# One change in three places of a two-layer decoder trunk: the attention's value products turned over, the router's products in column strips, and the first expert's tokens picked straight from x

## The reference

```python
def rmsnorm(x, g):
    y = xf * lax.rsqrt(jnp.mean(xf * xf, axis=-1, keepdims=True) + RMS_EPS)
    return y * g
# layer 0, attention: o_g = softmax(q k^T / 8, masked) v for 3 groups,
#   merged with weights softmax over groups of the log-sum-exps, then @ w_o
# layer 1, pooling mixer:
x = x + (window_mean(h) - h) @ w_group * scale
# layer 1, experts:
logits = h @ w_router                      # 256 x 8
top_val, top_idx = lax.top_k(logits, 2)
gates = softmax(top_val)
x = x + sum over the 2 chosen experts of gate * (silu(h Wg) * (h Wu)) Wd
```

## Time and profile before

| what | value |
|---|---|
| median of 3 runs | 1531.43 us |
| profiled execution | 1531.06 us, span 1529.3 us |
| PE busy | 1493.1 us (98%) |
| PEld busy | 1258.0 us (82%) |
| DVE busy | 1200.3 us (78%) |
| ACT busy | 965.2 us (63%) |
| attention | about 20 to 312 us of the span |
| dense layer | about 312 to 503 us |
| pooling, routing, first tokens | about 503 to 539 us |
| experts | about 539 to 1514 us |

### The profile page before, as it was taken

How to read it: one execution, slowest core, us unless ns; L and a number is a source line. 1 busy time by engine, 2 the same in 40 slices (tenths; PEclk the granted TensorE clock), 3 DMA queues, 4 the chain that set the end, 5 groups by cost and what they waited for, 6 DMA issues and landing times.

```text
span 1529.3 us, 20821 instructions
## 1 busy us (share of the span) xinstructions
PE 1493.1 (98%) x7818; PEld 1258.0 (82%) x7818; DVE 1200.3 (78%) x986; ACT 965.2 (63%) x801; POOL 115.8 (8%) x64
## 2 busy tenths in 40 slices
PE   6999999999999899999999999999999999999996
PEld 6999999878888878888888888888888888888885
DVE  6877677674455678888888888888888888888886
ACT  4444444454434667777777777777777777777775
POOL 2332232100000000000000000000000000000000
PEclk9999999999999999999999999999999999999999
DMA  9633343255557498999999999899899899999980
GB/s 376 213 139 138 139 138 139 83 200 193 189 173 271 149 354 342 367 378 366 377 355 401 350 371 395 353 355 400 345 367 393 345 377 381 360 377 363 393 318 30
DMA packets 66858, 449.33 MB, mean 294 GB/s; under 512 B 7648, under 2 KB 9440, under 8 KB 14448
## 3 DMA queue, kind: packets, MB, share of 16 engines
q1 hardware_dynamic: 63264, 439.84, 74.3%
q0 software_dynamic: 3392, 8.69, 2.2%
q10 hardware_dynamic: 144, 0.02, 0.0%
HBM read 440.65 MB, written 7.86 MB: 293 GB/s over the span
## 4 chain that ended last, share of the span: by engine, by line
PE 94%; DVE 3%; ACT 1%; DMA 1%; issue 0%; SPq 0%; DVEq 0%; ACTq 0%
PE bank L380 29%; PE bank L382 29%; PE bank L381 29%; PE bank L1362 2%; PE bank L1514 2%; DVE w_lo L328 1%; PE bank L1349 1%; PE bank L1339 1%; DMA raw<-in_units 1%; DVE rot L894 1%; PE bank L1523 0%; PE bank L1380 0%; PE bank L1445 0%; PE bank L1473 0%; ACT w_hi L323 0%
## 5 line engine op out<-in xcount | busy, mean ns | idle before, releaser
L328 DVE TENSOR_TENSOR w_lo<-raw,w_hi 128x2048 fp32r<-128x2048 f32 x201 | 460.0, 2291 | 137.1 <-ACT w_hi L323 135.6
L323 ACT ACTIVATE w_hi<-raw 128x2048 fp32r<-128x2048 f32 x201 | 384.7, 1915 | 146.5 <-PE bank L382 136.0
L380 PE MATMUL bank<-w_hi,xg_hi 128*128 128x512 f32 x896 | 358.8, 400 | 0.0
L381 PE MATMUL bank<-w_lo,xg_hi 128*128 128x512 f32 x896 | 354.4, 396 | 0.0
L382 PE MATMUL bank<-w_hi,xg_lo 128*128 128x512 f32 x896 | 354.3, 395 | 0.0
L328 DVE TENSOR_TENSOR w_lo<-raw_late,w_hi 128x2048 fp32r<-128x2048 f32 x95 | 217.7, 2292 | 45.9 <-ACT w_hi L323 44.7
L328 DVE TENSOR_TENSOR w_lo<-raw_more,w_hi 128x2048 fp32r<-128x2048 f32 x96 | 219.8, 2289 | 26.3 <-ACT w_hi L323 25.9
L323 ACT ACTIVATE w_hi<-raw_more 128x2048 fp32r<-128x2048 f32 x96 | 184.6, 1923 | 55.7 <-PE bank L382 55.7
L323 ACT ACTIVATE w_hi<-raw_late 128x2048 fp32r<-128x2048 f32 x95 | 182.2, 1918 | 34.1 <-PE bank L382 34.1
L382 PEld LDWEIGHTS bank<-w_hi,xg_lo 128*128 128x128 f32 x896 | 168.2, 188 | 41.1
L380 PEld LDWEIGHTS bank<-w_hi,xg_hi 128*128 128x128 f32 x896 | 168.5, 188 | 38.9
(11 more groups left out here) (200 smaller groups left out, 1835.2 us busy)
## 6 DMA issues: line engine op xcount, KB each, us to landing
raw<-in_expert_units SPq DMA_DIRECT2D x128, 1024.0 KB, 5.5
raw_more<-in_expert_units SPq DMA_DIRECT2D x96, 1024.0 KB, 5.5
raw_late<-in_expert_units SPq DMA_DIRECT2D x96, 1024.0 KB, 4.9
raw<-in_units SPq DMA_DIRECT2D x73, 1024.0 KB, 4.8
hn<-in_expert_units SPq DMA_DIRECT2D x16, 1024.0 KB, 6.8
qkT<-in_xT SPq DMA_DIRECT2D x2, 512.0 KB, 4.3
raw<-in_units SPq DMA_DIRECT2D x2, 512.0 KB, 6.9
x<-in_x SPq DMA_DIRECT2D x1, 1024.0 KB, 9.4
```

Source lines behind the costliest of these rows:

```text
L323: nc.scalar.activation(w_hi[:, u % SPLIT, :], where, ACT.Copy).then_inc(hi_ready, 1)
L328: nc.vector.tensor_tensor(w_lo[:, u % SPLIT, :], home(u, i)[0], w_hi[:, u % SPLIT, :].bitcast(F32), ALU.subtract).then_inc(lo_ready, 1)
L380: nc.tensor.matmul(bank, hi, w[0], start=start, stop=False)
L381: nc.tensor.matmul(bank, hi, w[1], start=False, stop=False)
```

## The change

In the attention, the "values" step exchanges its operands: v is now the stationary side (64 columns), eT moves (128 columns), and the two heads write to the two partition halves of one bank, so the output comes out already turned. The inverse sums, which were a column, are spread over a row block (DVE), turned by one PE transpose and copied back (DVE), and the turned output is multiplied with them into `out_T`. "turn out" on PE is gone; ACT and DVE split `out_T` from SBUF. DVE holds back its `split_lo` of unit n + 3 until it has done the turn, values or scores piece that follows.

At the end of the dense layer the pooling weights are scaled in four parts, and the square root's table is loaded before the last split. `keep_warm` has 6, 4 and 3 products instead of 10, 6 and 5. DVE adds pooled groups 2 and 3 before it splits the first expert unit, and splits it in two halves. PE turns x in four places between the pooling maps. The router is padded to 32 columns and is the stationary side, hT moves (256 columns), and the eight channel blocks use four column strips of 32; DVE copies the sums out and two small products with `fold` add the strips. Expert 0's tokens are picked by float32 products directly from x, with 1/rms in the picking matrix. `hn` is written by ACT without the norm weight; the weight is applied per channel when picked tokens are copied (`gathered_hi`, `picked_lo`: four instructions of 128 columns in place of one of 512, for all experts). Unit 1 of expert 0 comes before the overflow test and the slot sums. Loop iterations now begin at unit 2. The broadcast DMA of the norm weight is gone.

```diff
@@ sync @@
-                             (rows[:, 1, :], ffn_norm[1:2, :].to_broadcast([P, D])),
...
-                    10: (hnsplit_lo, 2 * TT)}
+                    10: (hn_ready, TT)}
@@ scalar @@
             def output_halves(c):
-                act.wait_ge(o_turned, c + 1)
-                nc.scalar.activation(a_hi[:, c * 512:(c + 1) * 512], ps[2][:, :], ACT.Copy).then_inc(a_hi_ready, 1)
+                cols = slice(c * 512, (c + 1) * 512)
+                act.wait_ge(o_ready, 4 * (c + 1))
+                nc.scalar.activation(a_hi[:, cols], out_T[:, cols], ACT.Copy).then_inc(a_hi_ready, 1)
...
+            load_table(ACT.Sqrt, 0)
             split_hi(act, U_MOE)
...
-            load_table(ACT.Sqrt, 0)
...
             root_of_tile(0)
+            act.wait_ge(rstd_ready, 3)
+            token_hi(0, 0)
             act.wait_ge(ffn_added, 3)
             square(2, 1, 0, 2)
-            act.wait_ge(rstd_ready, 3)
-            token_hi(0, 0)
...
-            act.wait_ge(unit_used, U_POOL + 1)
+            act.wait_ge(rstd_ready, 5)
             for t in range(TT):
-                act.wait_ge(hn_ready, t + 1)
-                nc.scalar.activation(a_hi[:, t * D:(t + 1) * D], hn[:, t, :], ACT.Copy).then_inc(hnsplit_hi, 1)
-            split_hi(act, U_MOE + 2)
+                nc.scalar.activation(hn[:, t, :], x[:, t, :], ACT.Copy, scale=rstd(3, t)).then_inc(hn_ready, 1)
...
             def gathered_hi(n):
-                nc.scalar.activation(xg_hi[:, 4 * n:4 * n + 4, :],
-                                     ps[(3, 5)[n]][:, :].rearrange("p (k s) -> p k s", k=4), ACT.Copy)\
-                    .then_inc(xg_hi_ready, 1)
+                for q in range(4):
+                    k = 4 * n + q
+                    nc.scalar.activation(xg_hi[:, k, :], ps[(3, 5)[n]][:, q * P:(q + 1) * P], ACT.Copy,
+                                         scale=gain_col[:, 3, k:k + 1]).then_inc(xg_hi_ready, 1)
...
             def round_of_experts(first):
+                if not first:
+                    softmax_exp()
                 gather(first)
                 if not first:
-                    softmax_exp()
+                    split_hi(act, U_MOE + 2)
@@ vector @@
+                if behind is not None and kind not in ("turn", "values", "scores"):
+                    split_lo(dve, behind)
+                    behind = None
...
                     if n < N_QKV - 1:
-                        split_lo(dve, n + 3)
+                        behind = n + 3
...
                 elif kind == "values":
                     c, pair, t = pair_of(n)
-                    at = (c * QH + 2 * pair) * HD
+                    at = (2 * c + pair) * SEQ + t * P
+                    dve.wait_ge(rinv_turned, n + 1)
+                    nc.vector.tensor_copy(rinv_T, ps[2][:, 0:P]).then_inc(rinv_T_ready, 1)
+                    dve.wait_ge(rinv_T_ready, n + 1)
+                    dve.wait_ge(pv_ready, n + 1)
+                    nc.vector.tensor_tensor(out_T[:, at:at + P], ps[7][:, 0:P], rinv_T, ALU.mult)\
+                        .then_inc(o_ready, 1)
+                elif kind == "turn":
                     dve.wait_ge(exp_ready, 2 * n + 2)
                     nc.vector.reciprocal(softs[:, n % 2, 3, :], softs[:, n % 2, 2, :]).then_inc(rinv_ready, 1)
                     dve.wait_ge(rinv_ready, n + 1)
...
+                    nc.vector.tensor_copy(spread.rearrange("p (a n) -> p a n", a=2),
+                                          softs[:, n % 2, 3, :].unsqueeze(2).to_broadcast([P, 2, HD])).then_inc(rinv_spread, 1)
...
-            split_lo(dve, U_MOE)
             for g in range(2, PG):
                 for t in range(TT):
                     add_pooled(g, t)
...
+            dve.wait_ge(hi_ready, U_MOE + 1)
+            first_unit_lo(0, first_half_lo)
+            dve.wait_ge(partial_ready, 1)
+            nc.vector.tensor_copy(partial, ps[0][:, 0:SEQ]).then_inc(partial_out, 1)
...
-            normed(3, 1)
...
-            pick_slots(0, 0)
-            for t, n in ((1, 0), (0, 1), (1, 1)):
-                normed_lo(t, n)
+            for t in range(TT):
+                nc.vector.tensor_scalar(pick_scaled[:, t, :], iota[:, 0:P], slot1[:, t, 0:1], rstd(3, t),
+                                        ALU.is_equal, ALU.mult).then_inc(scaled_ready, 1)
+            first_unit_lo(1, lo_ready)
...
             def picked_lo(i, n):
-                dve.wait_ge(xg_hi_ready, 2 * (i + 1) + n + 1)
-                nc.vector.tensor_tensor(xg_lo[:, 4 * n:4 * n + 4, :],
-                                        ps[(3, 5)[n]][:, :].rearrange("p (k s) -> p k s", k=4),
-                                        xg_hi[:, 4 * n:4 * n + 4, :].bitcast(F32), ALU.subtract).then_inc(xg_lo_ready, 1)
+                for q in range(4):
+                    k = 4 * n + q
+                    dve.wait_ge(xg_hi_ready, KD * (i + 1) + 4 * n + 4)
+                    nc.vector.scalar_tensor_tensor(xg_lo[:, k, :], ps[(3, 5)[n]][:, q * P:(q + 1) * P], gain_col[:, 3, k:k + 1],
+                                                   xg_hi[:, k, :].bitcast(F32), ALU.mult, ALU.subtract).then_inc(xg_lo_ready, 1)
...
                 else:
-                    gather(first, U_MOE + 1)
-                    split_lo(dve, U_MOE + 2)
                     softmax_weights()
+                    for n in range(2):
+                        picked_lo(-1, n)
+                    split_lo(dve, U_MOE + 1)
+                    pick_slots(0, 0)
                     chain(nc.vector.tensor_scalar(far, slot1[:, :, :], float(P), None, ALU.is_gt))
                     nc.vector.tensor_reduce(over[:, 0:1], far, AX.XY, ALU.add).then_inc(over_ready, 1)
...
+                    split_lo(dve, U_MOE + 2)
                     dve.wait_ge(overs_summed, 1)
@@ tensor @@
-                    for side in range(2):
-                        pe.wait_ge(eT_ready, 2 * n + side + 1)
-                        col = (2 * pair + side) * HD
-                        for k, (g, kt) in enumerate(((0, 0), (0, 1), (1, t), (2, t))):
-                            last = nc.tensor.matmul(ps[7][:, side * HD:(side + 1) * HD], eT[:, side, k * P:(k + 1) * P],
-                                                    v_sb[:, c % 2, g, kt, col:col + HD], start=k == 0, stop=k == 3)
+                    pe.wait_ge(rinv_spread, n + 1)
+                    nc.tensor.transpose(ps[2][:, 0:P], spread, ident[:, :]).then_inc(rinv_turned, 1)
+                    pe.wait_ge(eT_ready, 2 * n + 2)
+                    for k, (g, kt) in enumerate(((0, 0), (0, 1), (1, t), (2, t))):
+                        for side in range(2):
+                            col = (2 * pair + side) * HD
+                            last = nc.tensor.matmul(ps[7][side * HD:(side + 1) * HD, 0:P],
+                                                    v_sb[:, c % 2, g, kt, col:col + HD],
+                                                    eT[:, side, k * P:(k + 1) * P], start=k == 0, stop=k == 3)
...
+                    c = k % 4 * 32
+                    last = nc.tensor.matmul(ps[0][c:c + 32, 0:SEQ], router_g[:, k, :], hT[:, k, :], start=k < 4, stop=k >= 4)
...
-                    for t in range(TT):
-                        last = nc.tensor.matmul(ps[0][:, t * E:(t + 1) * E], hT[:, k, t * P:(t + 1) * P], router_g[:, k, :],
-                                                start=k == 0 and t == 0, stop=k == KD - 1, skip_group_check=True)
...
+            def first_gather():
+                pe.wait_ge(scaled_ready, TT)
+                for n in range(2):
+                    for q in range(4):
+                        for t in range(TT):
+                            c = (4 * n + q) * P
+                            last = nc.tensor.matmul(ps[(3, 5)[n]][:, q * P:(q + 1) * P], x[:, t, c:c + P],
+                                                    pick_scaled[:, t, :], start=t == 0, stop=t == TT - 1)
+                    last.then_inc(gather_ready, 1)
...
+                    first_gather()
+                unit(first, 0, False, first == 0)
+                unit(first, 1, False, first == 0)
                 if not first:
+                    pe.wait_ge(pick_ready, TT)
                     pe.wait_ge(over_ready, 1)
```

177 lines of the change are left out of this document (92 added, 85 removed).

## The result

The changed kernel takes 1490.34 us (median of 4 runs, 1490.07 to 1490.9) against 1531.92 us before in the same comparison (1531.42 to 1532.98). The ratio is 0.9728, interval 0.9711 to 0.9745: faster by 41.6 us.

The account below looks back on a forecast made before the run. PE was taken to bound attention and experts, with a chain through DVE and ACT between 503 and 539 us. Terms of -14.5 (attention), -6.7 and +3.2 gave -18.0 us: 1513.4 us, range 1507 to 1527.

Parts of the forecast that it names:

- Every change of expert ... +3.2 us: Experts: four small copies per half of picked tokens make PE wait some 0.45 us at each of seven changes, +3.2 us.
- Below 0 it can't go, as nothing is removed: Lower bound on the cost at expert changes: no gain possible there; the upper bound was +10.7 us.
- Values, -10.3 us: Attention values step: products pair in two column halves, so 16 steps take 18.8 us for 29.1, -10.3 us.
- Rivals 1 and 2: Attention values: 1, strips overlap nothing, even loads, +17.6 us, 1542.3, chance 7%; 2, strips serial, loads hidden, +3.1, 1527.8, 13%.
- "Turn out", -1.8: Attention: four times four transposes at 0.11 us leave PE, -1.8 us.
- Exponentials, -2.4: Attention: PE's waits for exponentials in five places go because DVE lets scores go ahead of its split, -2.4 us.
- From 503 us to the fourth unit, -6.7: Router, picking and start of experts: picking starts 2.8 us earlier, then 3.9 us more to the fourth unit, -6.7 us.
- Rival 3: Start of the experts gives half because the clock may stay low through picking: -3 for -6.7, 1517.1 us, chance 12%.
- Rival 4: Changes of expert: the small copies cost as much as those of 256 columns, +10.7 us, 1520.9 us, chance 8%.

## Why the prediction was wrong, step by step

- *"Every change of expert ... +3.2 us"*, and behind it the silent assumption that the other 960 us of the experts stay. **This is the step that failed.** The copies cost +4.3 at the addresses of before, which the forecast assumed, and +5.3 at the new ones (a mis-sized term: the wait was right, its echo in the next product was missing). The assumption failed by 21.6 us: the padding of `router_g` and the new `fold`, read only for what they do in the router, moved xg and hT onto multiples of 128 bytes. "Below 0 it can't go, as nothing is removed" was the false sentence. With the addresses as before the change gives 19.7 us (1511.93 against 1531.6), where I had forecast 18.0.
- The trace of before held the hint. These are rows of its dense layer (stationary side a_hi and a_lo, at multiples of 128), three records apart, the same shape and clock as in the experts:

```profile
399.15 0.39 PE L382 MATMUL bank<-w_hi,a_lo 128*128 128x512 f32 x1
...
399.83 0.39 PE L382 MATMUL bank<-w_hi,a_lo 128*128 128x512 f32 x1
```

  Three records in 0.68 us here, 0.70 in the experts. PE waits for nothing in either stretch, so the difference asked for a cause, and the prediction didn't look for one.
- *Values, -10.3 us.* Right in mechanism; 28.3 us for 16 steps became 19.7, -8.6. A step is 1.23 us wherever it stands; forecast were 1.09, and 1.29 with the return to the full array (18.8 us in all). The term that was too small is the change of the array's division: it takes 0.20 us from the transpose to the first pair and 0.20 from the last pair to what follows, where pairs are 0.11 apart, so some 0.09 each way at every step; I had counted it once at most steps. And 16 steps before had been taken at 1.82, while those without scores behind them take 1.70. Rivals 1 and 2 fall: pairs start 0.007 us apart and 0.109 us behind the last pair. The Trainium skill (TensorE: Matmul & The Clock Gate, Part 3) has a speedup of 2.38 for three column tiles, from which I had estimated 1.6 for two; measured is about 2, as pairs start 0.109 us apart and single products of one half do too (in the kernel with the heads apart). Its rule that a weight load overlaps running products only where the row group differs isn't borne out either: column halves share their row group, and 16 records start within 0.82 us, with their loads (0.14 us each in the profile) under the products.
- *"Turn out", -1.8.* Right in size (16 transposes, 1.7 us from start to start before), and all of it is gone from PE.
- *Exponentials, -2.4.* 3.9 alone (3.6 of it at the exponentials), and 9.9 in the company of the other edits. The three attention edits are not a sum. Values and turn out without the held-back split gave 4.8 us up to the first landmark (307.4 us for 312.1). The steps on PE are shorter then, and DVE has the spread copy besides (forecast 0.2 us, 0.79 on the average, as most are held up by POOL), so PE waits in more places. How the 9.9 divide between these two, no run shows.
- *From 503 us to the fourth unit, -6.7.* 9.9. The order was read rightly: the overflow answer behind two units was worth 7.9 as it ran (5.3 at the full clock is the estimate). Of the 3.2 us that it gave beyond the forecast, 1.1 are the low clock that I had allowed for at the picking and that didn't come. Another 1.8 came before the picking: measured from the first filler, the logits' copy came 1.0 us earlier than forecast, the slots behind it 0.5 (2.2 us for 2.7) and the picking behind those 0.3 (0.9 for 1.2). Rival 3, that it gives half, falls.
- *Rival 4, small copies as dear as 256 columns:* falls (1.12 us for four); the cost of +5.3 came from elsewhere.

What stays open: why a multiple of 128 bytes counts. The moving side was not tried by itself, nor were products of fewer than 512 columns with a misaligned stationary side in a stream that PE bounds; in the attention aligning made no difference, but no product there that has 512 columns began off such a multiple.

## What to carry to other kernels

Read a change's declarations for the addresses that they move, and where one trace has two spacings for one shape at one clock, look for what differs before you forecast: here it was worth as much as the rest of the change (21.6 and 19.7 us). A term worked out for one edit alone holds only where the next edit doesn't put new work in front of it. An idle engine is no free one while it locks out the engine on the path.

## What the runs showed of the hardware

- A stream of 512-column products on rounded float32 operands goes at 0.227 to 0.228 us each if the stationary operand begins at a multiple of 128 bytes in its partition, and at 0.2333 at 32, 64 and 96 past one (a difference of 2.4%).
- Products in the two column halves of the array pair up (starts 0.007 us apart, the next pair 0.109 us later), and about half of them still do if four of one half are issued ahead of four of the other (1.51 us for 1.03).
- After a short wait of PE the second product of 512 columns starts 0.33 in place of 0.23 us behind the first, 0.10 us more per wait; at transposes each short wait cost 0.16 us more than the idle time shown for it.
- Going from the full array to halves of it, or back, costs PE some 0.09 us (0.20 us between starts for 0.11).
- POOL and DVE hold each other up for whole instructions that work in SBUF: an addition of 1.5 us took 3.4 on POOL behind a split on DVE, and a small multiplication of 0.18 us took 2.17 on DVE beside POOL.
